# A value product in two column halves, denominators summed on VectorE and an evenly spread maximum pass in a causal attention stage

## What is computed

```python
def fox_attend(q, c_q, q_pos, k, v, c_k):
    s = jnp.einsum('bqhd,bkhd->bhqk', q, k).astype(jnp.float32) * (HEAD_DIM ** -0.5)
    s = s + jnp.swapaxes(c_q, 1, 2)[..., :, None] - jnp.swapaxes(c_k, 1, 2)[..., None, :]
    causal = jnp.arange(k.shape[1])[None, :] <= q_pos[:, None]
    s = jnp.where(causal, s, -jnp.inf)
    p = jax.nn.softmax(s, axis=-1)
    return jnp.einsum('bhqk,bkhd->bqhd', p.astype(v.dtype), v)
```

## Time and profile before

| what | before |
|---|---|
| median of three runs | 4107.84 us |
| span of the profiled execution | 4106.5 us |
| first score matmul (L1027) to the last value product (L1011) | 1259.6 to 2717.5 us |
| one head, the five of the loop | 241.8 to 252.6 us |
| the last head | 228.3 us |

### The profile page before, as it was taken

One profiled execution on the slowest core, in us unless ns is written; L12 is line 12 of the kernel. 1 busy time (PEld: TensorE's weight loads), 2 busy tenths in 40 slices (PEclk: granted clock), 3 DMA queues, 4 the chain that ended last, 5 costly groups with the idle time before them and its releaser, 6 DMA issues. The chain is left out here.

```text
span 4106.5 us, 45401 instructions
## 1 busy us (share of the span) xinstructions
PE 3573.2 (87%) x14504; PEld 2549.9 (62%) x14504; DVE 1689.6 (41%) x2594; ACT 1011.2 (25%) x1823; POOL 651.6 (16%) x1265
## 2 busy tenths in 40 slices
PE   5999999999968989989999999967777775498999
PEld 4987988979844555555555555534335652376766
DVE  4122122131117657465573746527625442323232
ACT  1102111121112443434334343423201110112120
POOL 0000000000027777700000000000036630000000
PEclk9998999989977999999999999988777676698989
DMA  3232232132231121210101001032245532332422
GB/s 103 93 118 82 78 134 81 55 132 91 74 71 47 67 68 48 79 40 16 38 20 34 21 19 27 8 120 54 49 143 175 170 97 92 119 115 92 122 85 72
DMA packets 234113, 323.61 MB, mean 79 GB/s; under 512 B 100548, under 2 KB 168812, under 8 KB 232372
## 3 DMA queue, kind: packets, MB, share of 16 engines
q1 hardware_dynamic: 184436, 203.79, 17.6%
q10 hardware_dynamic: 37584, 68.48, 4.5%
q0 software_dynamic: 11904, 48.87, 3.4%
HBM read 221.37 MB, written 99.61 MB: 78 GB/s over the span
## 5 line engine op out<-in xcount | busy, mean ns | idle before, releaser
L1011 PE MATMUL bank<-p,vone 128*128 128x512 f32 (+1 forms) x1728 | 861.9, 581 | 10.5 <-ACT p L958 9.9
L958 ACT ACTIVATE p<-bank,ncol 128x512 f32<-128x512 f32 (+1 forms) x864 | 562.1, 651 | 815.4 <-PE bank L1028 645.7
L1027 PE MATMUL bank<-qhi,kst 128*128 128x512 f32 (+1 forms) x864 | 644.2, 746 | 14.0 <-issue 12.6
L879 DVE TENSOR_REDUCE pm<-bank 128x1 f32<-128x512 f32 (+2 forms) x864 | 516.8, 640 | 261.0 <-PE bank L998 193.0
L1011 PEld LDWEIGHTS bank<-p,vone 128*128 128x128 f32 x1728 | 320.9, 198 | 73.6 <-issue 13.1
L478 DVE CAST whi<-wraw 128x3072 fp32r<-128x3072 f32 (+2 forms) x32 | 52.1, 1629 | 755.9 <-PE bank L539 755.9
L998 PE MATMUL bank<-kone,qone 66*128 66x512 f32 (+2 forms) x864 | 293.6, 412 | 59.8 <-DVE qlo L865 33.9
L539 PE MATMUL bank<-xhi,whi 128*128 128x512 f32 x832 | 332.0, 399 | 6.9 <-DVE xlo L504 6.9
L1028 PE MATMUL bank<-qlo,kone 66*128 66x512 f32 (+1 forms) x864 | 335.9, 389 | 0.0
L539 PE MATMUL bank<-xhi,wlo 128*128 128x512 f32 x832 | 331.3, 398 | 0.0
L539 PE MATMUL bank<-xlo,whi 128*128 128x512 f32 x832 | 330.9, 398 | 0.0
(11 more groups left out here) (390 smaller groups left out, 4970.7 us busy)
## 6 DMA issues: line engine op xcount, KB each, us to landing
wraw<-in_w_in SPq DMA_DIRECT2D x20, 1536.0 KB, 6.8
ssm_consts<-gp POOLq DMA_DIRECT2D x6, 3080.0 KB, 10.0
x_tok<-in_x_prompt SPq DMA_DIRECT2D x8, 2048.0 KB, 12.6
gate_t<-fstage ACTq DMA_DIRECT2D x32, 512.0 KB, 2.6
mx_x<-in_x_prompt SPq DMA_DIRECT2D x32, 512.0 KB, 3.5
out_y_prompt<-mx_xo ACTq DMA_DIRECT2D x32, 512.0 KB, 2.9
q<-q_t SPq DMA_DIRECT2D x96, 128.0 KB, 3.1
past_k<-in_cache_k POOLq DMA_DIRECT2D x64, 192.0 KB, 3.3
```

What stands on the lines that cost most here:

```text
L879: dve.tensor_reduce(pm[:, r, ch:ch + 1], c.bank[XB + n % NPRE][:, 0:w], AX.X, ALU.max).then_inc(pre_max, 1)
L958: act.activation(p[:, n % 3, q0:512], c.bank[n % SB][:, q0:512], ACT.Exp, bias=ncol[:, j:j + 1]).then_inc(ex, 1)
L1011: pe.matmul(c.bank[OB + b % 2][:, q0:512], vone[:, j, :], p[:, n % 3, q0:512], start=(j == 0), stop=(j == 4 * b + 3), skip_group_check=Tru ...
L1027: pe.matmul(bank[:, q0:512], kst[:, j * P:(j + 1) * P], qhi[:, b % QS, q0:512], start=True, stop=False)
```

## The change

The stage is written out over all 864 tiles, without a loop over heads; `FoxPlan` makes the order. A value product is two matmuls of 64 stationary columns (`vt`, values alone) by 256 moving columns, one into partitions 0 to 63 and one into 64 to 127 of the result bank. The denominators are made on VectorE, which adds every `p` to `acc` (`add_up`); at the end of a block two matmuls with ones sum `acc` over the partitions into the upper 256 columns of the bank (`denominators`). `finish` then works on 128 x 256 in place of 64 x 512. The chunks of the maximum pass are placed at tile m*100/122 - 16 of their head, m counting the chunks. `p` has four buffers, ScalarE's bias comes from `c.negc` with no copy, `split_k` works on four tiles at a time, gates are loaded one block ahead, and gate loads and stores are two DMAs a block.

```diff
+class FoxPlan:
+    def __init__(self, nh, nb, lead, num, den):
...
+        for g in range(self.blocks):
+            h, b = divmod(g, nb)
+            when = [max(-1, self.per * h + (m * den) // num - lead) for m in range(self.start[b], self.start[b + 1])]
+            for m, t in zip(range(self.start[b], self.start[b + 1]), when):
+                self.chunks_at.setdefault(t, []).append(self.per * h + m)
+            self.rows_at.setdefault(when[-1] + 2 if when[-1] >= 0 else -1, []).append(g)
+            self.split_at.setdefault(max(-1, when[0] - 3), []).append(g)
...
+    QS, PS, GS = 4, 4, 4
+    plan = FoxPlan(NF, NB, 16, 122, 100)
...
-        vone = sb("vone", [P, NT, P])
-        gate = sb("gate_a", [HD, T])
-        p = sb("p", [P, 3, 512])
+        vt = sb("v_tok", [P, NT, HD])
+        gate = sb("gate_a", [P, GS, 256])
+        p = sb("p", [P, PS, 512])
+        acc = sb("acc", [P, 2, 512])
...
VectorE
+            def add_up(n):
+                h, b, j, q0 = plan.tile(n)
+                g = NB * h + b
+                dve.wait_ge(ex, n + 1)
+                if j == 0:
+                    if g >= 2:
+                        dve.wait_ge(den, g - 1)
+                    dve.tensor_copy(acc[:, g % 2, :], p[:, n % PS, :]).then_inc(acc_done, 1)
+                else:
+                    dve.wait_ge(acc_done, n)
+                    dve.tensor_tensor(acc[:, g % 2, q0:512], acc[:, g % 2, q0:512], p[:, n % PS, q0:512], ALU.add
+                                      ).then_inc(acc_done, 1)
+            def finish(g):
+                ob = c.bank[OB + g % 2]
+                dve.wait_ge(den, g + 1)
+                dve.reciprocal(rec[:], ob[:, 256:512]).then_inc(o_rec, 1)
+                dve.wait_ge(o_rec, g + 1)
+                dve.tensor_tensor(on[:], ob[:, 0:256], rec[:], ALU.mult).then_inc(o_norm, 1)
...
+                dve.tensor_tensor(og[:, g % 2, :], on[:], gate[:, g % GS, :], ALU.mult).then_inc(o_gated, 1)
...
+            for n in range(NMN):
+                if n:
+                    add_up(n - 1)
+                for m in plan.chunks_at.get(n, []):
+                    maximum(m)
+                for x in plan.rows_at.get(n, []):
+                    row(x)
+                for x in plan.split_at.get(n, []):
+                    split_q(x)
+                if j == 2 and n > 4:
+                    finish(g - 1)
...
ScalarE
+                if n >= PS:
+                    act.wait_ge(pv, n - PS + 1)
+                    act.wait_ge(acc_done, n - PS + 1)
...
TensorE
+            def weighted(n):
...
+                pe.wait_ge(ex, n + 1)
...
+                for hf in range(2):
+                    lo, hi = max(q0, 256 * hf), 256 * (hf + 1)
+                    if lo < hi:
+                        mm = pe.matmul(c.bank[OB + g % 2][HD * hf:HD * (hf + 1), lo - 256 * hf:256], vt[:, j, :], p[:, n % PS, lo:hi],
+                                       start=(j == 0), stop=(j == 4 * b + 1 + 2 * hf), skip_group_check=True)
+                mm.then_inc(pv, 1)
+            def denominators(g):
+                pe.wait_ge(acc_done, plan.end(g))
+                for hf in range(2):
+                    mm = pe.matmul(c.bank[OB + g % 2][HD * hf:HD * (hf + 1), 256:512], c.ones[:, 0:HD],
+                                   acc[:, g % 2, 256 * hf:256 * (hf + 1)], start=True, stop=True, skip_group_check=True)
+                mm.then_inc(den, 1)
...
+            for n in range(NMN):
...
+                for m in plan.chunks_at.get(n, []):
+                    first_pass(m)
+                for x in plan.rows_at.get(n, []):
+                    maxima_to_rows(x)
+                if n:
+                    weighted(n - 1)
+                if j == 2 and n > 4:
+                    denominators(g - 1)
+                if b == NB - 1 and h + 1 < NF and j and j % KG == 0:
+                    turn_k(h + 1, j // KG - 1)
...
SyncE
+                for g in (plan.rows_at.get(n - 1, []) if n else []):
+                    m_row(g)
...
+                if j == 3 and n > 4:
+                    store(NB * h + b - 1)
```

More of the change, by code:

```diff
@@ L711, in fox_prompt @@
     SB, XB, NPRE, TB, OB = 2, 2, 3, 5, 6
[L713 to L721, removed]
+    QS, PS, GS = 4, 4, 4
+    plan = FoxPlan(NF, NB, 16, 122, 100)
+    NMN, PER, NBLK = plan.total, plan.per, plan.blocks
     with ExitStack() as s:
@@ L760, in fox_prompt, with load_k @@
         block = s.enter_context(nc.Block())
[L762 to L766, removed]
         @block.sync
         def _(sp):
[L770 to L773, removed]
+            def load_k(h):
+                sp.dma_start(ktok[:], k_h[h]).then_inc(k_in, 16)
@@ L785, in store @@
-            def store(h, b):
-                sp.wait_ge(o_gated, NB * h + b + 1)
-                sp.sem_inc(s_turn, 1)
[L788 to L811, removed]
@@ L816, in _ @@
+            load_k(0)
+            load_q(0)
+            load_q(1)
             sp.wait_ge(ones_set, 5)
@@ L818, in _ @@
                 load_vc(0, g)
[L819 to L828, removed]
+            for g in plan.split_at[-1][2:]:
+                load_q(g)
+            loaded = len(plan.split_at[-1])
+            for g in plan.rows_at[-1]:
+                m_row(g)
@@ new lines, in _ @@
+            for g in range(2):
+                load_gate(g)
+            for n in range(NMN):
+                h, b, j, q0 = plan.tile(n)
+                r = n % PER
+                for g in plan.split_at.get(n + 3, []) + (sum((plan.split_at.get(x, []) for x in range(-1, 3)), []) if n == 0 else []):
+                    while loaded <= min(g + 1, NBLK - 1):
+                        load_q(loaded)
+                        loaded += 1
+                if r == 100 and h + 1 < NF:
+                    sp.wait_ge(khl_done, 2 * NG * (h + 1))
+                    load_k(h + 1)
+                for g in (plan.rows_at.get(n - 1, []) if n else []):
+                    m_row(g)
+                if b == NB - 1 and h + 1 < NF and j % KG == 1 and j > KG:
+                    load_vc(h + 1, j // KG - 1)
+                if j == 0:
+                    g = NB * h + b
+                    if g + 1 < NBLK and g:
+                        load_gate(g + 1)
+                if j == 3 and n > 4:
+                    store(NB * h + b - 1)
+                if r == PER - 1 and h + 1 < NF:
+                    load_vc(h + 1, NG - 1)
@@ L943, in _ @@
+            add_up(NMN - 1)
+            finish(NBLK - 1)
         @block.scalar
@@ L1066, in _ @@
[L1066 to L1079 removed]
+                turns[0] += 1
@@ new lines, in weighted @@
+            def weighted(n):
+                h, b, j, q0 = plan.tile(n)
+                g = NB * h + b
+                pe.wait_ge(ex, n + 1)
+                if j == 0 and g >= 2:
+                    pe.wait_ge(o_norm, g - 1)
+                for hf in range(2):
+                    lo, hi = max(q0, 256 * hf), 256 * (hf + 1)
[3 more added lines that the diff above has]
+                mm.then_inc(pv, 1)
```

377 lines of the change are left out of this document (178 added, 199 removed).

## The result

The changed kernel takes 4231.1 us (median of four runs, 4208.2 to 4246.85) against 4108.06 before: a ratio of 1.0299, 95% interval 1.0263 to 1.0335. It is 3.0% slower. The forecast was 4088, and the range ended at 4215. The profiled run took 4246.85, the slowest of the four.

A forecast was written before the change was run, and what follows sets the result against it. TensorE was taken to bound the stage, VectorE the first two heads: 2 x 265 + 4 x 226 - 8 = 1426, plus 14 loss, 1440 against 1458; with the last closing, 4106.5 - 20 = 4086.5, median-adjusted 4088 us; range 4015 to 4215.

The forecast's parts named there:

- the loss: Hand-overs between two equally loaded engines behind three banks: 1.5% of the four clean heads, 14 us.
- block 2 at a granted clock of 0.86: Profile before: 24.7 us for 12 tiles, 2.06 a tile, read as VectorE holding TensorE up.
- the clean heads: Heads without GpSimd beside them: 226 us each, four of them, the last 8 us shorter.
- the first two: Heads with GpSimd building its tables beside them: 265 us each, VectorE the bound there.
- The product: Value product of a full tile: 0.86 to 0.78 us, halves run at once (0.43) plus 0.35 for changing tiling.
- the rival of halves in a row: Value product's column halves don't run at once: about 4180 us in part, about 4300 not at all; chance 0.14.
- The blocks: Blocks 0 to 7 of a clean head: 9, 14, 20, 25, 30, 37, 40 and 51 us, a head 226.
- TensorE's own work in a head: Matmul work per head stays at 221 us; only the 22 us lost can be won.
- VectorE: Its load per head goes from 145 to 203 us, 92% of TensorE's 221; 251 us beside GpSimd.
- GpSimd's company: First two heads: a VectorE sum costs 0.31 us more beside GpSimd, 42 us a head on 136 sums.
- the rival by which VectorE becomes the bound everywhere: Sums at 0.68 us in place of 0.60 cost 11 us a head: 4153 us; chance 0.18.
- The even pass: Maximum-pass chunks spread at 1.22 a tile: TensorE 1.53 us a tile, VectorE 1.33 plus 3.7 a block.

The follow-up runs named there:

- the tables held: The changed kernel with GpSimd's tables held back until the last value product, so they do not run beside the stage: stage 1464.0 us, whole 4582.4.
- narrow sums: The changed kernel with each of VectorE's sums over 4 columns in place of 512: 4058.4 us (one run).
- the rounding of q: Two of three q-split instructions moved to ScalarE, against whole products in heads 0 and 1, then half products two tiles together: 3970.4 us, ratio 0.9665.
- one wait put in by hand: The changed kernel with sums over 4 columns, plus one TensorE wait for VectorE before tile 88 of the fourth head: 4081.7 us (one run).

## Why the prediction was wrong

**The step that failed** is the loss: "some is lost at each hand-over; I add 1.5% of the four clean heads, 14 us". The forecast priced a wait as the time waited, and every other term at full clock. The waits are indeed no more than that, 3.0 us a clean head, 1.2%. But one of them takes the clock with it, and with it 29.4 us, ten times the waits of the whole head. The sign stood in the rows: block 2 at a granted clock of 0.86, read there only as a place where VectorE holds TensorE up. In the sum: the clean heads were put at 4 x 226 - 8 + 14 = 910 us and took 1002.3 (+92), the first two at 530 and took 606.2 (+76), together the 168.5 between the forecast stage of 1440 and the measured 1608.5. The first two heads spend some 325 us at the lower clock by their windows (0.80 and 0.67); at what the one fall cost, 29.4 us for 68.2, that would be 140 us, an estimate and more than the 76. Why one wait takes the clock and an equal one doesn't stays open.

**The product** was priced right. A tile without a chunk in the last block, at full clock (timeline of TensorE):

```profile
2835.16 0.65 PE L1050 MATMUL bank<-p,v_tok 128*64 128x256 f32 x4
...
2836.40 0.65 PE L1050 MATMUL bank<-p,v_tok 128*64 128x256 f32 x4
```

The four half matmuls run in pairs, 0.65 us in all. From product to product it is 1.24 us; the forecast had 1.25, of which the product was 0.78; with the forecast's 0.23 and 0.24 for the scores it is 1.24 - 0.47 = 0.77. That rules out the rival of halves in a row.

**The blocks** came out as forecast wherever the clock stayed up: the second head with the tables held took 223.3 us at a clock of 1.00; the forecast was 226. TensorE's own work in a head, put at 221 (its terms add up to 220), is 218.6 with narrow sums.

**VectorE** was put at 203 us a clean head and measured 205.7. Beside GpSimd it was put at 251 and measured 239 and 228; one sum was busy for 0.81 us there on average and 0.63 later (all shapes), within its bounds: GpSimd's company, put at 0.31 a sum, was 0.17. The rival by which VectorE becomes the bound everywhere isn't what happened either: TensorE waits 3.0 us for it in a clean head.

**The even pass** with the small parts was worth 44 us, more than the 20 forecast for all parts together.

So the rivals on the slow side were two, and what came true was neither. A third was missing: what does a wait cost besides its own length? The Trainium skill's page "TensorE: Matmul & The Clock Gate" (What's actually happening) says that the clock is held down by default and that activity releases it. The traces agree that the clock falls behind waits, here of 0.9 and 0.3 us; that TensorE, recorded busy without a gap, then stays at 0.50 for 68.2 us is not what this rule would give, and here the measurement decides. The Trainium skill's page "TensorEngine Tiling (Array Packing)" (Tiling Modes), which the forecast cites, has every change of mode drain the engine. The traces agree with that in the 0.36 us a tile of two changes; that products with fewer changes win the clock back sooner is shown by the runs above.

## What to carry to other kernels

A wait on TensorE costs its own length and whatever the clock does after it, so read the granted clock of each stretch beside the waits: a stage with fewer waits can be slower. Before splitting a matmul over halves of the array among whole ones, issue the halves of several tiles together; here two tiles at a time gave 22.6 us a head in tiling time (218.6 to 196) and brought the longest stretch at the lower clock from 136 us (the changed kernel's second head) down to 24. And where an engine is to be loaded to over nine tenths of the other, first take work from it at the places where its bursts lie, as with the rounding of q.

## What the runs showed that was not expected

- A granted clock of 0.50 for 68.2 us, and in a run with one wait put in by hand for 78.5 us, in which the profile shows TensorE busy (68.20 of 68.20 us in the first). A busy share of 100% thus says nothing of the clock.
- The same wait of 0.89 us, with the same instructions around it, once with a fall of the clock behind it and once without, 29.4 us apart.
- Half the changes of tiling gave 0.16 us a tile ((218.6 - 196) / 144), a little under half of the 0.35 that the rows of the memory stage had given for one product; whole products, two tiles together, gave nothing.
